# First projection in seven half-size block products instead of full dense tiles

## What is computed

```python
z = x @ w["w_in"]
gq, gk, gv, gr, ga, sq, sk, sv, mq, gl = jnp.split(z, SPLIT_AT, axis=-1)
log_a = jax.nn.log_sigmoid((ga @ w["w_gla_a2"] + w["b_gla_a"]).astype(jnp.float32)) / GLA_TAU
```

## Time and profile before

| what | us |
|---|---|
| median of the runs | 1777.29 |
| the profiled execution | 1777.36 |
| its span | 1775.5 |
| TensorE matmul busy in the span | 1750.6 |
| VectorE, ScalarE, GpSimd busy | 1001.9, 716.7, 231.7 |

### The profile page before, as it was taken

One profiled execution on the slowest core, in us unless ns is written; L12 is line 12 of the kernel. 1 busy time (PEld: TensorE's weight loads), 2 busy tenths in 40 slices (PEclk: granted clock), 3 DMA queues, 4 the chain that ended last, 5 costly groups with the idle time before them and its releaser, 6 DMA issues.

```text
span 1775.5 us, 31156 instructions
## 1 busy us (share of the span) xinstructions
PE 1750.6 (99%) x11872; PEld 1695.5 (95%) x11872; DVE 1001.9 (56%) x1379; ACT 716.7 (40%) x1272; POOL 231.7 (13%) x324
## 2 busy tenths in 40 slices
PE   8999999999999999999999999999999999999997
PEld 7999999999999799989998889999999999999997
DVE  3111165555242766657656688777777677554464
ACT  3222244343222555554332245545444454433342
POOL 0000000000020200000000014333333331002011
PEclk9999999999999999999999999999999999999999
DMA  5111122122422411124454232222222223885662
GB/s 176 48 47 36 46 67 84 60 88 66 118 58 72 128 50 48 33 75 136 133 181 143 82 91 74 72 86 81 79 77 72 72 72 107 260 266 165 214 228 73
DMA packets 181451, 180.30 MB, mean 102 GB/s; under 512 B 21021, under 2 KB 149086, under 8 KB 181374
## 3 DMA queue, kind: packets, MB, share of 16 engines
q1 hardware_dynamic: 179518, 173.24, 32.1%
q0 software_dynamic: 1856, 5.99, 0.9%
HBM read 143.08 MB, written 35.53 MB: 101 GB/s over the span
## 4 chain that ended last, share of the span: by engine, by line
PE 94%; DVE 3%; issue 1%; ACT 1%; DMA 1%; POOL 0%; SPq 0%; ACTq 0%; POOLq 0%; DVEq 0%
PE banks L1462 24%; PE banks L1028 19%; PE banks L1029 18%; PE banks L1030 18%; PE banks L1419 5%; PE banks L1256 1%; PE banks L1273 1%; PE banks L1236 1%; PE banks L1268 1%; PE banks L1241 1%; DMA x_rows<-in_x_prompt 0%; PE banks L1136 0%; PE banks L1148 0%; PE banks L1142 0%; PE banks L1430 0%
## 5 line engine op out<-in xcount | busy, mean ns | idle before, releaser
L1028 PE MATMUL banks<-act_hi,w_hi 128*128 128x352 f32 (+1 forms) x1200 | 395.9, 330 | 1.3 <-DVE act_lo L2124 1.3
L1030 PE MATMUL banks<-act_hi,w_lo 128*128 128x352 f32 (+1 forms) x1200 | 390.1, 325 | 0.0
L1029 PE MATMUL banks<-act_lo,w_hi 128*128 128x352 f32 (+1 forms) x1200 | 389.9, 325 | 0.0
L2113 DVE TENSOR_TENSOR w_lo<-w_raw,w_hi 128x1024 fp32r<-128x1024 f32 x70 | 87.3, 1248 | 317.4 <-ACT w_hi L1565 317.4
L1028 PEld LDWEIGHTS banks<-act_hi,w_hi 128*128 128x128 f32 x1200 | 226.9, 189 | 6.1 <-issue 2.4
L1462 PE MATMUL banks<-x_free_r,a_hi 128*128 128x256 f32 x1232 | 226.8, 282 | 0.8 <-DVE a_lo L2449 0.5
L1029 PEld LDWEIGHTS banks<-act_lo,w_hi 128*128 128x128 f32 x1200 | 226.8, 189 | 0.4
L1030 PEld LDWEIGHTS banks<-act_hi,w_lo 128*128 128x128 f32 x1200 | 226.7, 189 | 0.0
L1462 PEld LDWEIGHTS banks<-x_free_r,a_hi 128*128 128x128 f32 x1232 | 190.1, 188 | 1.3 <-DVE x_free_r L2475 0.7
L1462 PE MATMUL banks<-xs_hi,a_hi 128*128 128x274 f32 x616 | 178.8, 290 | 1.7 <-DVE xs_lo L2475 1.0
L1462 PE MATMUL banks<-xs_lo,a_hi 128*128 128x274 f32 x616 | 178.4, 290 | 0.0
(11 more groups left out here) (314 smaller groups left out, 3335.2 us busy)
## 6 DMA issues: line engine op xcount, KB each, us to landing
w_raw<-in_w_down SPq DMA_DIRECT2D x112, 256.0 KB, 3.4
w_raw<-in_w_in SPq DMA_DIRECT2D x100, 256.0 KB, 3.3
gate_in<-gates_scratch SPq DMA_DIRECT2D x24, 529.0 KB, 3.8
h_keep<-conv SPq DMA_DIRECT2D x22, 530.0 KB, 2.7
w_raw<-in_w_up SPq DMA_DIRECT2D x44, 256.0 KB, 3.8
x_free<-in_w_up SPq DMA_DIRECT2D x44, 256.0 KB, 3.6
h_raw<-h_keep SPq DMA_DIRECT2D x22, 384.0 KB, 5.1
gates_scratch<-gate_st SPq DMA_DIRECT2D x32, 176.0 KB, 1.9
```

What stands on the lines that cost most here:

```text
L1028: pe.matmul(out, hi, b_hi, start=start, stop=False)
L1029: pe.matmul(out, hi, b_lo, start=False, stop=False)
L1030: return pe.matmul(out, lo, b_hi, start=False, stop=stop)
L2113: dve.tensor_tensor(dst[:, :, :], w_raw[slot][:, :, :], src[:, :, :].bitcast(F32), ALU.subtract).then_inc(q.w_split_lo, 1)
```

## The change

The tiles are taken in pairs of 256 output features. A pair's weights are four blocks of 512 x 128, its tokens two halves, and seven products of sums of blocks give the four output blocks that eight plain products would. This is done in windows `n` = 0 to 13, one pair and one token slice each. Windows 0 to 6 take pairs 1 to 7 over the first 512 tokens (halves of 256), windows 7 to 13 take pairs 0 to 6 over the last 548 (halves of 274; the slices overlap by two columns). Pair 0 of the first slice and pair 7 of the second stay dense (`z_dense`), in front of and behind the windows. In each window the weights are loaded, summed and split anew.

The raw weights keep the two slots `w_raw`, which together now hold the four blocks of one window: upper and lower half of slot 0, upper and lower half of slot 1. GpSimd makes sum 1 (both halves of slot 1), sum 2 (sum 1 less slot 0's upper half), sum 3 (slot 0's upper half less slot 1's) and sum 4 (slot 0's lower half less sum 2). ScalarE makes seven high parts, VectorE seven low parts, called split 0 to 6 here; splits 0 and 3 are of slot 0, 6 of slot 1's lower half, and 1, 2, 4, 5 of sums 1 to 4. Four partial results are copied out by ScalarE (snaps), three are added by VectorE (combines). The token side needs four sums and four splits per slice, on VectorE and, in part, on GpSimd (`t_step`). The input rows land in a part of `z` in place of `x_rows`, tiles 4 to 8 are turned inside windows 0 to 2, and the small forget-gate constants are loaded at the end of the stage.

```diff
+Z_BASE, Z_HALF = (0, TT - 548), (256, 274)
+Z_FIRST = (0, 3, 1, 2, 4, 5, 6)
+Z_PREP = (0, 1, 2, 3, 4, 6, 5)
+Z_FIRST_PREP = (0, 3, 1, 2, 4, 6, 5)
+Z_SUMS = (1, 2, 4, 6)
+NZ = 14
...
+    ZA_AT = (R_AT + 8192, R_AT + 12288, R_AT + 20480, R_AT + 16384, B_AT, B_AT + 4096, B_AT + 8192)
+    za_hi = [at(f"za_hi{j}", [P, 4, P], F32R, offset=ZA_AT[j]) for j in range(NA)]
+    za_lo = [at(f"za_lo{j}", [P, 4, P], F32R, offset=ZA_AT[j] + 2048) for j in range(NA)]
+    za_f = {j: at(f"za_f{j}", [P, 4, P], F32, offset=ZA_AT[j] + 2048) for j in (1, 4)}
...
+        def x_load(t):
+            w = tok(t)[1]
+            src = I["x_prompt"][0, t * P:(t + 1) * P, :] if t < NT else I["x_sample"][0]
+            row = 8 + 2 * (t % 4)
+            if t >= 4:
+                sp.wait_ge(q.rows_turned, t - 3)
+            sp.dma_start(z[0:w, row:row + 2, 512:1024], src.rearrange("t (r c) -> t r c", r=2)).then_inc(x_landed[X_GROUP[t]], 16)
+        def z_block(n, m, i):
+            sp.dma_start(z_raw(m, i), w_in[:, 4 * i:4 * i + 4, bass.ds(z_pair(n) * 256 + m * P, P)]).then_inc(w_landed[m], 16)
+        def z_load(n):
+            sp.wait_ge(q.a_summed, n * 4)
+            sp.wait_ge(q.a_lo_done, n * NA - 3)
+            z_block(n, 1, 0)
+            z_block(n, 0, 0)
+            z_block(n, 0, 1)
+            sp.wait_ge(q.a_lo_done, n * NA - 1)
+            z_block(n, 1, 1)
+        x_load(0)
+        x_load(1)
+        cols(0, 0, w_in, C_GQ)
+        cols(0, 1, w_in, C_GQ + P)
+        x_load(2)
+        x_load(3)
+        for m in range(2):
+            sp.wait_ge(q.w_split_lo, m + 1)
+            for i in range(2):
+                z_block(0, m, i)
+        for t in range(4, 8):
+            x_load(t)
...
+        z_load(1)
+        x_load(8)
+        for n in range(2, 9):
+            z_load(n)
+        with sp.Fori(9, NZ) as n:
+            z_load(n)
...
-        with sp.Fori(1, 8) as i:
-            for j in range(2):
-                cols(i, j, w_in, i * 256 + C_GQ + j * P)
...
+        def z_sums12(n):
+            first = isinstance(n, int) and n == 0
+            s1 = za_first if first else za_f[1][:, :, :]
+            pool.wait_ge(w_landed[1], z_landed(n))
+            if not first:
+                pool.wait_ge(q.prod_mm[0], z_prod(n - 1, 1))
+            pool.tensor_tensor(s1, z_raw(1, 0), z_raw(1, 1), ALU.add).then_inc(q.a_summed, 1)
+            pool.wait_ge(w_landed[0], z_landed(n))
+            if not first:
+                pool.wait_ge(q.a_lo_done, z_prep(n - 1, 5))
+            pool.wait_ge(q.a_summed, n * 4 + 1)
+            pool.tensor_tensor(za_sum[:, :, :], s1, z_raw(0, 0), ALU.subtract).then_inc(q.a_summed, 1)
+        def z_sum3(n):
+            if not (isinstance(n, int) and n == 0):
+                pool.wait_ge(q.prod_mm[0], z_prod(n - 1, 4))
+            pool.tensor_tensor(za_f[4][:, :, :], z_raw(0, 0), z_raw(1, 0), ALU.subtract).then_inc(q.a_summed, 1)
+        def z_sum4(n):
+            pool.wait_ge(q.a_lo_done, z_prep(n, 2))
+            pool.tensor_tensor(za_sum[:, :, :], z_raw(0, 1), za_sum[:, :, :], ALU.subtract).then_inc(q.a_summed, 1)
...
+        for n in range(7):
+            z_sums12(n + 1)
+            if n == 3:
+                pool.wait_ge(q.x_lo_done, x_count(8))
+                t_step(0, t1, t_quarter(act_hi, 0, 1), t_quarter(act_hi, 0, 0), ALU.subtract)
+            if n == 4:
...
+        with pool.Fori(8, NZ) as n:
+            z_sums12(n)
+            z_sum3(n)
+            z_sum4(n)
...
+        def z_product(n, par, s, j, beside=None):
+            first = isinstance(n, int) and n == 0
+            early = isinstance(n, int) and n < 2
+            a, b, c = z_banks(par)
+            w = Z_HALF[s]
+            pe.wait_ge(q.a_lo_done, z_prep(n, j))
+            if isinstance(n, int) and n in (0, 7) and j in Z_SUMS:
+                pe.wait_ge(q.x_lo_done, z_sum_count(s, j))
+            if first and j == 0:
+                pe.wait_ge(q.x_summed, 10)
+            if not first and early and j == 0:
+                pe.wait_ge(q.proj_free, PS_Z)
+            if not early and j == 0:
+                pe.wait_ge(q.snapped[0], n * 4 - 4)
+            if not early and j == 1:
+                pe.wait_ge(q.combined[0], n * 3 - 3)
+            if not early and j == 3:
+                pe.wait_ge(q.combined[0], n * 3 - 5)
+            if j == 2:
+                pe.wait_ge(q.snapped[0], n * 4 + 1)
+            if j == 4:
+                pe.wait_ge(q.snapped[0], n * 4 + 3)
+            if j == 5:
+                pe.wait_ge(q.snapped[0], n * 4 + 2)
+            if j == 6:
+                pe.wait_ge(q.combined[0], n * 3 + 2)
+            if j in Z_SUMS:
+                x_hi, x_lo = (t[s][Z_SUMS.index(j)][:, :, :] for t in (zt_hi, zt_lo))
+            else:
+                x_hi, x_lo = (z_plain(t, s, j) for t in (act_hi, act_lo))
+            fresh = j in (0, 1, 3)
+            out = bank(b if j in (1, 5) else c if j == 3 else a)[:, 0:w]
+            for k in range(4):
+                for n_, (l, r) in enumerate(((za_hi, x_hi), (za_hi, x_lo), (za_lo, x_hi))):
+                    last = pe.matmul(out, l[j][:, k, :], r[:, k, :], start=fresh and k == 0 and n_ == 0,
+                                     stop=k == 3 and n_ == 2, skip_group_check=True)
+            last.then_inc(q.prod_mm[0], 1)
...
-        with pe.Fori(1, 7) as i:
-            proj_tile(i, 0, i * 6, 0)
-            proj_tile(i, 1, i * 6 + 3, 1)
-        proj_tile(7, 0, 42, 0)
...
+        for n in range(8):
+            z_pair_products(n, 1 - n % 2, n // 7, besides.get(n, {}))
+        with pe.Fori(4, NZ // 2) as i:
+            for b in range(2):
+                z_pair_products(i * 2 + b, 1 - b, 1)
...
+        def z_split(n, j):
+            first = isinstance(n, int) and n == 0
+            if j in (0, 3, 6):
+                m = j // 6
+                act.wait_ge(w_landed[m], z_landed(n))
+                src = z_raw(m, int(j > 0))
+            else:
+                act.wait_ge(q.a_summed, n * 4 + {1: 1, 2: 2, 4: 3, 5: 4}[j])
+                src = za_sum[:, :, :] if j in (2, 5) else za_first if first and j == 1 else za_f[j][:, :, :]
+            if first:
+                if j < 4:
+                    act.wait_ge(q.proj_done, 3 if j in (0, 3) else 4)
+            else:
+                act.wait_ge(q.prod_mm[0], z_prod(n - 1, j))
+            act.activation(za_hi[j][:, :, :], src, ACT.Copy).then_inc(q.a_hi_done, 1)
...
+        def z_window(n, par, s, p, prep=True, mid=None, end=None):
+            z_split(n, 6)
+            z_snap(n, par, s, p, 0)
+            z_split(n, 5)
+            z_snap(n, par, s, p, 1)
+            z_snap(n, par, s, p, 2)
+            if mid:
+                mid()
+            if prep:
+                for j in range(5):
+                    z_split(n + 1, j)
+            if end:
+                end()
+            z_snap(n, par, s, p, 3)
...
+        def z_tile_sums(t):
+            c, done = (t - 2) * P, 5 * (t - 2)
+            cols = slice(c, c + P)
+            s1, s2, s3 = (zt_sum[0][i][:, :, cols] for i in range(3))
+            upper, lower = x_bank(t)[:, 0:4, :], x_bank(t)[:, 4:8, :]
...
+        def z_low(n, j):
+            dve.wait_ge(q.a_hi_done, z_prep(n, j))
+            first = isinstance(n, int) and n == 0
+            if j == 1:
+                dve.wait_ge(q.a_summed, n * 4 + 2)
+            if j in (0, 3, 6):
+                src = z_raw(j // 6, int(j > 0))
+            else:
+                src = za_sum[:, :, :] if j in (2, 5) else za_first if first and j == 1 else za_f[j][:, :, :]
+            dve.tensor_tensor(za_lo[j][:, :, :], src, za_hi[j][:, :, :].bitcast(F32), ALU.subtract).then_inc(q.a_lo_done, 1)
...
+        def z_combine(n, par, s, p, k):
+            a, b, c = z_banks(par)
+            dve.wait_ge(q.prod_mm[0], z_prod(n, (3, 4, 5)[k]))
+            dve.wait_ge(q.snapped[0], n * 4 + (k + 1))
+            out = z_out(s, p, *((0, 0), (1, 1), (0, 1))[k])
+            dve.tensor_tensor(out, bank((c, a, b)[k])[:, 0:Z_HALF[s]], out, ALU.add).then_inc(q.combined[0], 1)
+        def z_window(n, par, s, p, prep=True, mid=None, end=None):
+            z_low(n, 6)
+            z_low(n, 5)
+            if mid:
+                mid()
+            if prep:
+                z_low(n + 1, 0)
+                z_low(n + 1, 1)
+            z_combine(n, par, s, p, 0)
+            z_combine(n, par, s, p, 1)
+            if prep:
+                z_low(n + 1, 2)
+                z_low(n + 1, 3)
+            z_combine(n, par, s, p, 2)
+            if prep:
+                z_low(n + 1, 4)
+            if end:
+                end()
```

424 lines of the change are left out of this document (308 added, 116 removed).

## The result

The changed kernel takes 1830.41 us, the median of four runs between 1829.76 and 1831.37. The kernel before takes 1777.21 beside it. The ratio is 1.030, with a 95% interval of 1.0282 to 1.0318: 3% slower. The forecast was 1834, its range 1796 to 1856.

What follows compares the result with a forecast made beforehand. TensorE bounded the old stage; the new load-and-sum loop would bound it: 40.2 + 183.3 + 17.5 + 3.4 + 9.6 + 21.8 = 275.8 against 216.06 us, less 3 at the start, so 1777.4 + 57 = 1834 us, range 1796 to 1856.

Steps and rivals of the forecast that it cites:

- The loop sets the stage: Windows: sum 4 frees slot 0, next load, splits and sums lead to the next sum 4; 13 rounds, 183.3 us.
- the token steps: Windows 4 to 7: seven GpSimd steps of 2.5 us between sums 2, 3 and 4, all in the round, 17.5 us.
- The round of 14.1: Each window, end of sum 4 to end of sum 4: wake, load, splits, sums and two combines add to 14.1 us.
- The exclusion: VectorE instructions with two SBUF inputs and GpSimd instructions reading SBUF exclude each other, so splits and sums count in one line.
- the second rival: The loop bounds, but sums and splits overlap: rounds of 11.8 us, stage +19 us, 1796 us; chance 14%.
- The wait before product 6: Every window: TensorE waits some 3.5 us for the second combine, which stands behind split 1 of the next window.
- The switch round: Around window 8: VectorE's two long second-slice token operations before split 0, with ScalarE's part, add some 3.4 us.
- Start and end: Sum 4 of window 0 ends at 40.2 us; after the last, matmuls 9.6, then dense tiles, forget gate and waits 21.8.
- an exclusion that falls the other way: At the start, window 0's three sums may wait instead of VectorE: up to 3.9 us off, 3 taken.
- the third rival: TensorE falls to its lower clock behind the windows' gaps: up to +102 us, 1879, mixtures from 1850 up; chance 10%.
- The gain of 17.9 us: Stage matmuls: TensorE's spacing falls from 186.6 to 168.7 us, so TensorE alone gains 17.9 us.
- the first rival: TensorE stays the bound, with rounds of 10 us: stage ends at 202, 14 us gained, 1763 us; chance 6%.

Runs made afterwards that it cites:

- the run with one SBUF operand: Changed kernel, but from window 8's last two splits on VectorE multiplies the high part by a PSUM bank of zeros instead of computing low parts; 1822.87 us, ratio 1.0253.
- Switch only: Kernel with all sums and token steps on VectorE and load cut in two (1780.32 us), token splits at the slice switch moved earlier; 1776.13 us, ratio 0.9996.

## Why the prediction came out right

- **The loop sets the stage.** Shown. Leaving out the load takes 42 us, cutting it in two 17, the combines 9, the sums' engine 22, the token steps 11. None of them touches a matmul.
- **The round of 14.1.** Rounds 1 to 3 and 9 to 13 take 112.7 us against 8 x 14.1 = 112.8; single ones lie between 13.7 and 14.4. Inside it, the load ran from 223.43 (end of sum 4) to 230.15, 6.7 us; the prediction had 0.15 + 5.0 + 0.63 + 0.60 = 6.4 for the same stretch. There it was split 0 that sum 1 waited for; here it starts at the landing by record and then takes 1.52 us, of which 0.25 are the rest of split 0. In four of the 13 rounds the view names TensorE's product 1 of the window before as what released sum 1, and not the landing. GpSimd is idle for 5.7 to 7.0 us in these and for 5.6 to 6.8 in the others, so little of any round hangs on it.
- **The exclusion.** Shown from two sides: it goes with the second SBUF operand, and it comes back with the token steps. This is the second rival's case; its rounds of 11.8 appeared nowhere, and the run with one SBUF operand, which has what that rival assumed, gave 12.8. One reading is looser than the prediction has it: of the two combines at 1141.85 the first began ahead of the sum at 1142.09, so those rows show only the second one under a sum. The run with one SBUF operand shows it cleanly.
- **The wait before product 6**, put at 3.5 us, is 3.7.
- **The term that was mis-sized is the token steps**, by 5.4 us. The prediction took all seven into the round, 17.5 us. They last 17.4 (2.13 to 2.97 each), but the four rounds are only 68.5 - 4 x 14.1 = 12.1 longer. The second step of a window stands between sums 3 and 4, where GpSimd is idle for 1.93 us in the other windows: that much was covered. The fourth of these windows has no second step, and its round is 1.9 longer than 14.1, against 3.0 to 4.3 in the others. Moving the steps shortened the four rounds by 11.0, a second measure of the term.

```profile
93.67 1.72 POOL L1004 TENSOR_TENSOR za_f<-w_raw,w_raw 128x512 f32<-128x512 f32 x1
95.35 2.97 POOL L1014 TENSOR_TENSOR z<-z,act_lo 128x1096 f32<-128x1096 f32 x1
98.28 1.74 POOL L1008 TENSOR_TENSOR za_sum<-w_raw,za_sum 128x512 f32<-128x512 f32 x1
```

- **The switch round.** It was put at 14.1 + 3.4 = 17.5 and is 16.8. Four us of such a round could be had by order alone, so the 3.4 was about the right size for a reason that the prediction gave only in part (ScalarE's splits of the token sums stood behind three copies of window 7).
- **Start and end.** Sum 4 of window 0 ends at 38.19 + 2.26 = 40.45 (put at 40.2), which is partly luck. The third tile was copied at 17.28 and not at 14.5, since its turn stood behind six matmuls of the first dense product, and these had waited until 12.87 for VectorE's low part of the weights. In exchange the exclusion held VectorE's tile sums up by 1.6 us (two of them are recorded at 1.20 and 1.75 in place of 0.68) and not by 3.9. The 3 us taken off for an exclusion that falls the other way did not come. From the last sum 4's end, 237.83, to 270.89 it is 33.1 us against 9.6 + 21.8 = 31.4; the clock, below, is the reason for most of this. The errors are +0.3, -6.8 (rounds), +1.7 and +3, in sum -1.9 on the stage (54.8 against 56.7, rounded to 57 in the forecast), and the 2 us behind it are the rest of 1834 - 1830.4. That the stage comes within 2 us is in part errors that cancel.
- **The clock** was the third rival. It stood at 0.90 in the mean over the stage and 0.77 in the worst 30 us, and not low throughout; with the waits gone it is back at 1.00. The slow matmuls stand behind the wait before product 6, and most of them fit into the slack before the next such wait. Behind the last one, 3.48 us long, nothing follows to take them up (windows view, TensorE's granted clock third from the end):

```profile
235.50:238.80 3.30, 3.25 (x14) 3.25 (x15) 2.88 (x4) 0.16 (x1) 1.66 (x1) 0.52 0.00 0
239.00:244.00 5.00, 5.00 (x41) 5.00 (x40) 1.39 (x2) 2.43 (x7) 0.00 (x0) 1.00 0.74 208
```

At 0.52, near the 1.2 GHz level, the matmuls of 274 columns stand 0.23 us apart, and at 1.00, the 2.4 GHz level, 0.127 as in the forecast. The 15 slow ones cost 1.6 us, about the 1.7 by which the end of the stage was late. The third rival put the same price on one slow piece and had it fit into the waits everywhere.

The gain of 17.9 us on TensorE's own work was collected in no run. With all of it the stage would have ended near 202, by the first rival's estimate, which nothing here shows. Switch only ends it at 216.7, where the kernel before ends at 216.06. Its rounds take 146.2 us against 6 x 10.04 + 7 x 10.67 = 134.9: the last five are TensorE's price (52.7 against 53.4), the first eight, with the token work, cost 12 us more than theirs (93.5 against 81.6).

## What to carry to other kernels

Trading matmuls for sums and splits pays only if the whole cycle from "buffer free" to "buffer free" is shorter than the matmuls it feeds, and that cycle is a sum over engines, not a maximum: here 14.1 us of steps against 10 of matmuls, with no other engine having more than about 6 us of work of its own in a window (in the profile after VectorE shows 7.6 of 14.3, its waits for GpSimd included). Add up such a cycle before the busy times, put side work of other engines where its owner waits for a load, and release each block of a buffer at its own last reader.

Two engines that hold each other off do not add up to more. Moving the sums from GpSimd (1.27 to 1.7 us each) to the busier VectorE (0.69) made the kernel faster, and work left on GpSimd beside it stretched VectorE's instructions from 0.69 to 2 to 3 us. And once two engines are near full, as VectorE and TensorE in the last runs, edits of order that each look sound cancel.

## What the runs showed that I had not expected

GpSimd's token step of 1096 elements per partition takes between 2.13 and 2.97 us, and the VectorE operation with two SBUF operands recorded beside a step up to 3.0 in place of 0.69: the two took turns, one instruction each, for as long as both had work. The kernel without loads shows the sum of it, 28.10 and 25.35 us busy in the same 30.

An edit of the same kind can be worth 9 us and nothing: the combines moved forward gave 9.3 us in the changed kernel, and, moved forward once more when VectorE was nearly full, no gain (1.2 us more, within the two intervals).

The fourth input tile is turned only at 20.65, although its own load, issued at 7.3, had landed 6.3 us later: tiles 3 and 4 (counted from 0) report on one semaphore, and TensorE waits for both, the second of which the change issues at 14.94, behind window 0's weights. It landed 5.7 us later. The change had turned a shared count into a wait; VectorE stood idle for 0.46 us before that tile's low part, so it cost little here.
